# Result rows loaded inside the experts stage, and the two rows of a token added by identity products on TensorE

## The reference, cut to what matters

```python
h = h + y                                        # mixer's output
h = h + hmoe(rmsnorm(h, ln_ffn[layer]), *moe)    # experts, both layers
# hmoe: a token goes to 2 of 32 experts
#   y[token] = sum over its two experts e of
#              c[token, e] * (silu(x @ w_gate[e]) * (x @ w_up[e])) @ w_down[e]
...
return rmsnorm(h, ln_out), ...
```

## Time and profile before

| | |
|---|---|
| times of three runs | 2485.36, 2490.96 (median), 2492.52 us |
| the profiled execution's own time | 2487.45 us |
| its span, first to last instruction | 2485.8 us |
| mean granted TensorE clock | 0.915 of full |
| DMA | 409.74 MB, mean 165 GB/s |

### The profile page before, as it was taken

One profiled execution on the slowest core, in us unless ns is written; L12 is line 12 of the kernel. 1 busy time (PEld: TensorE's weight loads), 2 busy tenths in 40 slices (PEclk: granted clock), 3 DMA queues, 4 the chain that ended last, 5 costly groups with the idle time before them and its releaser, 6 DMA issues. The chain is left out here.

```text
span 2485.8 us, 44144 instructions
## 1 busy us (share of the span) xinstructions
PE 2110.0 (85%) x17339; PEld 1368.9 (55%) x17339; DVE 900.7 (36%) x1763; ACT 487.0 (20%) x1120; POOL 462.1 (19%) x548
## 2 busy tenths in 40 slices
PE   3899989998953999957987888799999975799993
PEld 2678789994752333326876555455555565233333
DVE  4655247743122111224133666434363022112123
ACT  1311112221011111101001555433343000111100
POOL 0144022220003233320002333000000001323322
PEclk7999999997865999978998999999999895899996
DMA  1498340001252999922440100555547416599952
GB/s 56 144 294 272 113 164 4 6 36 42 68 175 88 374 374 396 373 91 60 112 132 23 32 1 2 177 185 161 184 144 238 148 22 240 215 374 372 394 205 103
DMA packets 238894, 409.74 MB, mean 165 GB/s; under 512 B 56770, under 2 KB 194595, under 8 KB 212436
## 3 DMA queue, kind: packets, MB, share of 16 engines
q1 hardware_dynamic: 191140, 346.48, 38.8%
q0 software_dynamic: 40288, 56.12, 7.3%
q10 hardware_dynamic: 7264, 4.36, 0.6%
HBM read 499.03 MB, written 81.57 MB: 234 GB/s over the span
## 5 line engine op out<-in xcount | busy, mean ns | idle before, releaser
L1619 PE MATMUL banks<-slots,work 128*64 128x512 f32 x1536 | 342.6, 599 | 0.0
L2592 PE MATMUL banks<-slots 128*128 128x508 f32 x512 | 249.2, 601 | 8.7 <-ACT work L2692 7.3
L1619 PEld LDWEIGHTS banks<-slots,work 128*64 128x64 f32 x1536 | 106.2, 138 | 202.7 <-issue 201.8
L909 PE MATMUL banks<-slots 64*64 64x64 f32 x5632 | 188.9, 224 | 23.7 <-issue 7.2
L909 PEld LDWEIGHTS banks<-slots 64*64 64x64 f32 x5632 | 185.1, 140 | 25.8 <-issue 13.9
L671 PE MATMUL banks<-slots,work 128*128 128x260 f32 x768 | 175.3, 387 | 4.6 <-DMA z_state<-in_consts 4.6
L1645 PE MATMUL banks<-slots,work 128*64 128x512 f32 x768 | 175.3, 598 | 3.6 <-DVE work L1697 3.6
L2663 DVE COPY slots<-banks 64x256 f32<-64x256 f32 x256 | 109.2, 426 | 166.8 <-PE banks L2498 162.5
L1891 PE MATMUL banks<-slots,work 128*128 128x260 f32 x640 | 150.0, 397 | 18.0 <-PEq L251 16.2
L671 PEld LDWEIGHTS banks<-slots,work 128*128 128x128 f32 x768 | 145.9, 192 | 32.7 <-issue 6.2
L1331 POOL DMA_INDIRECT expert_lists<-work x20 | 19.6, 981 | 770.0 <-DVEq L251 764.5
(11 more groups left out here) (416 smaller groups left out, 3012.5 us busy)
## 6 DMA issues: line engine op xcount, KB each, us to landing
slots<-in_moe_wgate SPq DMA_DIRECT2D x64, 1024.0 KB, 9.1
slots<-in_moe_wup SPq DMA_DIRECT2D x64, 1024.0 KB, 11.6
slots<-in_moe_wdown SPq DMA_DIRECT2D x64, 1024.0 KB, 11.3
sample_cache_rows<-in_cache_kv POOLq DMA_DIRECT2D x128, 256.0 KB, 4.5
slots<-in_cache_kv SPq DMA_DIRECT2D x256, 128.0 KB, 2.2
slots<-sample_cache_rows SPq DMA_DIRECT2D x32, 512.0 KB, 6.5
slots<-sample_cache_rows SPq DMA_DIRECT2D x64, 256.0 KB, 5.0
slots<-expert_result_rows SPq DMA_DIRECT2D x8, 1024.0 KB, 9.1
```

What stands on the lines that cost most here:

```text
L909: last = nc.tensor.matmul(out[half, k, :], block_of(i, u, left)[half, k, :], moving[half, :], start=(x == 0), stop=(x == len(terms) - 1))
L1619: last = mm(c.bank[v][SEAT * j:SEAT * j + SEAT, :], xt[v][:, k, SEAT * j:SEAT * j + SEAT], weights.gate_up_of[2 * s + j][:, k], start=(k = ...
L2592: last = mm(HIDDEN[:, 0:KVH * NCMP_S], s.w1[:, u // NB, j, :], s.xt[u % 2][:, :, j % 8, first:first + NCMP_S], start=(j == 0), stop=(j == 15))
```

## The change

The loads move to the end of SP's program in `experts`, behind a wait for all scatters. POOL's own wait for the scatters and its additions go. PE multiplies both rows of a token by the identity and lets the two products accumulate in PSUM, 16 products for a tile in place of 8 transposes. DVE's additions to `h` stay as they are. The rows now lie in slots 4 to 6, and the stage `combine` is gone.

```diff
     with c.stage(f"experts{layer}") as st:
...
+        rows_loaded = [st.sem(f"rows_loaded{n}") for n in range(NTILE)]
+        summed, added = st.sem("sums_in_psum"), st.sem("sums_added")
...
         def _(sp):
...
+            sp.wait_ge(finished, PAIRS - 1)
+            for v in range(2):
+                sp.wait_ge(scattered[v], 16 * PAIRS // 2)
+            for n in range(NTILE):
+                m = P if n < TT else NB
+                two = c.expert_rows[2 * P * n:2 * P * n + 2 * m].rearrange("(p a) e -> p a e", a=2)
+                sp.dma_start(pairs[0:m, n], two).then_inc(rows_loaded[n], 16)
...
         def _(pool):
...
-            for v in range(2):
-                pool.wait_ge(scattered[v], 16 * PAIRS // 2)
...
         def _(pe):
...
+            for n in range(NTILE):
+                m = P if n < TT else NB
+                pe.wait_ge(rows_loaded[n], 16)
+                if n >= 2:
+                    pe.wait_ge(added, 2 * (n - 1))
+                for k in range(KT):
+                    for a in range(2):
+                        last = mm(c.bank[2 * (n % 2) + k // 4][:, P * (k % 4):P * (k % 4) + m],
+                                  pairs[0:m, n, a, P * k:P * k + P], c.ident[0:m, 0:m],
+                                  start=(a == 0), stop=(a == 1))
+                last.then_inc(summed, 1)
...
         def _(dve):
...
+            # the additions to h of combine, waiting for `summed`
...
-def combine(c, layer):
...
     experts(c, layer, weights)
-    combine(c, layer)
```

More of the change, by code:

```diff
@@ L1539, in experts @@
     share = c.job_lists.bitcast(F32)
+    h, NTILE = c.slot(0), TT + 1
+    pairs = c.flat(4, 3)[:, 0:NTILE * 2 * D].rearrange("p (n a e) -> p n a e", a=2, e=D)
     with c.stage(f"experts{layer}") as st:
@@ L1648, in _ @@
                 last.then_inc(finished, 1)
+            for n in range(NTILE):
[6 more added lines that the diff above has]
+                        last = mm(c.bank[2 * (n % 2) + k // 4][:, P * (k % 4):P * (k % 4) + m],
+                                  pairs[0:m, n, a, P * k:P * k + P], c.ident[0:m, 0:m], start=(a == 0), stop=(a == 1))
+                last.then_inc(summed, 1)
         @block.scalar
@@ L1707, in _ @@
                 dve.drain().then_inc(weighted, 1)
-def combine(c, layer):
[L1712 to L1721, removed]
             for n in range(NTILE):
                 m = P if n < TT else NB
[L1724 to L1751, removed]
+                dve.wait_ge(summed, n + 1)
                 for a in range(2):
```

## The result

The changed kernel takes 2482.99 us (median of 20 runs, 2476.49 to 2490.52) against 2491.95 for the kernel before (20 runs, one of them 4446.40, which doesn't move the median). The ratio is 0.9963 with a 95% interval of 0.9951 to 0.9974: 9 us faster, 6.5 to 12. I had said 21.4 us, and the time lies outside the range given. Twelve more runs gave 2488.14 against 2491.79, ratio 0.9987 (0.9972 to 1.0003), which alone would not be told from no change.

What follows compares the result with a forecast made beforehand. The stretch around combine was taken to be bound by POOL's 7.90 us drain, which nothing needs before the next stage. Load start 16.6, chain 3.8 and norm 1.0 gave 21.4 us off 2490.96: 2469 us, range 2462 to 2478.

Steps and rivals of the forecast that it cites:

- The load's start: Between experts and combine: SP's first load starts 8.3 us earlier in each layer, 16.6 us gained in all.
- rival B: At the scatters' end: the load's start doesn't move, held by what holds POOL's drain; 2486 us, chance 4%.
- The drain hidden: At the end of experts: POOL's drain runs beside the loads, over by 1099.6, some 10 us before the stage's end.
- The transfers: Loads of the rows: unchanged at 2.4 us a tile; tile 0 lands 6.1 us (layer 0) and 4.8 (layer 1) after first load.
- The clock's rise: PE's products in the sum: 4.5 us at half clock (21 products), then full clock.
- PE's work: Adding rows on PE: 16 products a tile, each costing what a transpose costs, 0.112 us at full and 0.215 at half clock.
- the chain: First load to DVE's last addition: 18.0 us for 19.96 in layer 0, 17.05 for 18.97 in layer 1; 3.8 gained.
- The norm: Norm after the additions: its products gain up to 3.3 us if the clock is still up; 1.0 us taken.
- The sum: Whole kernel: 16.6 + 3.8 + 1.0 = 21.4 us gained, giving 2469 us.
- A: Rival on PE's products: the clock stays at half and PE sets the pace; 9.1 us gained, 2482 us, chance 8%.
- C: Rival on PE's products: an f32 product costs four times a transpose; slower, 15.7 us lost a layer, 2522 us, chance 3%.

Runs made afterwards that it cites:

- the joined version with POOL's additions: Changed kernel, early loads kept, but POOL adds the two rows and PE does 8 transposes a tile, all within experts: 2487.02 us, ratio 0.9985.
- the second profile: The changed kernel run and profiled once more without an edit; its twelve runs gave 2488.14 us against 2491.79, ratio 0.9987.

## Why the prediction was wrong, step by step

*The load's start*: right. It is 8.30 us earlier in each layer, as worked out (2.16 us behind the scatter's issue in place of 10.46), and with that rival B falls. *The drain hidden*: right in the changed kernel, over 18 us ahead. What I didn't see is that this hangs on POOL having nothing left to do behind its last scatter: in the joined version with POOL's additions the drain is paid after all.

*The transfers*: right in layer 1, tile 0 at 4.75 us. In layer 0 it landed at 4.9, not at 6.1, which gave 1.2 us; why isn't shown. In the run with `combine` a stage of its own and the products alone it was 6.3 again.

*The clock's rise*: right in kind, 3.4 us of products at half clock where I took 4.5; in layer 1 of the second profile it was 6.0.

*PE's work*: this step failed. "So a product costs what a transpose costs" rested on line 1938, 64 records in 7.30 us, read as 64 products. The program has 2 x 16 products there; the row counts two instructions for each. The page of before could have told it: the transposes of line 1607 are 8 a job in the code and x384 = 48 x 8 on the page, the gate and up products of line 1619 are 16 a job and x1536, which is 48 x 16 x 2:

```profile
L1619 PE MATMUL banks<-slots,work 128*64 128x512 f32 x1536 | 342.6, 599 | 0.0
...
L1607 PE MATMUL banks<-base_constants,work 128*128 128x128 f32 x384 | 55.9, 292 | 67.5 <-DMA work<-expert_token_rows,job_lists 65.0
```

I made the same mistake with lines 360, 1346 and 1928: their 32, 16 and 64 records are 16, 8 and 32 products, and a norm has 16 products, not the 32 that I gave it ahead of the prediction.

The price of a product is 0.223 us at full and 0.427 at half clock (15 records in the window of 3.4 us, 0.213 apart). Both lie just under the upper bounds that I had from the norm's products, 0.228 and 0.455; I took the near end, 0.112 and 0.215. The mean, 19.85/80 = 0.248 us, is below the 0.27 from which I had the change come out slower, and above what the transfers hide. With it the chain is 4.9 us to the landing of tile 0, 3.4 at half clock, then 145 x 0.1117 = 16.2, and 0.5 of additions: 25.0 from the first load, as measured in layer 0. So this step brings -5.1 and -5.9 us in place of +1.9 twice. The run with half of the products confirms the rest of the sum but for the norm: 20 us gained for 21.4 said, by its profile 16.6 of the loads' start, 3.7 of the chain (3.8 said) and 0.2 of the norm (1.0 said); the run with the products alone confirms the term by itself.

The Trainium skill had it, nearly: "FP8 and Floating Point Precision", section TensorE Precision Notes, gives true FP32 four passes. I set the rule of its page "TensorE: Matmul & The Clock Gate", section Terms, aside since 0.112 stood against 0.110 per record. This trace shows a product at twice the price of a transpose, 0.223 against 0.110 us, not at 4 times.

*The norm*: wrong in sign in the first profile. The clock falls just ahead of the norm's first product and is at half until 1121.7, 6.1 us behind the norm's first product. Before, it came up within 1123 to 1126, some 3 us behind the first product at 1120.73:

```profile
1120.00:1123.00 3.00, 2.27 (x5) 1.85 (x6) 2.53 (x4) 2.94 (x5) 0.00 (x0) 0.50 0.55 155
1123.00:1126.00 3.00, 3.00 (x13) 2.49 (x12) 0.00 (x0) 0.56 (x1) 0.00 (x0) 0.85 1.13 322
```

So the norm's products take 10.32 and 10.27 in place of 8.84 and 9.03. That is 2.7 us lost where I had 1.0 gained. It differs from run to run: in the second profile it is 8.71 and 8.73, 0.4 us gained.

*The sum* with these: 16.6 - 11.0 - 2.7 = 2.9 us in the profiles of before and after, and 16.6 - 13.6 + 0.4 = 3.4 with the second profile of the changed kernel. The medians say 9.0 (6.5 to 12.2) and 3.6 (-0.7 to 7.0). Of the 6.4 us between the spans of before and after the rest lies in stretches whose code is the same. The second profile of the changed kernel, at 2484.9 us of span, doesn't have these gains, so no lasting gain elsewhere is shown. The traces bear out some 3 us as the change's own; where the rest of the 9 comes from stays open.

*The rivals*: A's time was right, 2482, by luck: the clock did rise. C's mechanism, a product dearer than a transpose, is what happened, at twice and not four times. That the change came out faster at all is due to the loads: their 16.6 us are more than the products lose.

## What to carry to other kernels

Count a row's records against the calls in the code before its mean is taken for the price of a call; here an f32 product is two records and an f32 transpose one. Before an addition moves to another engine, ask which one has time for it inside the pace that is left: PE had not, but DVE took the sums at 1.23 us a tile and the chain fell to the pace of the transfers. A drain of POOL behind many indirect DMAs is a term of its own. It comes behind POOL's last instruction of the stage, so put transfers beside it, and leave what POOL would do with their data to the next stage or to another engine.

## What the runs showed of the hardware that I had not expected

A drain of POOL takes 7.90 us at the end of the experts stage, to the nanosecond the same in both layers, though no DMA is in flight. POOL has issued 96 indirect DMAs by then, 24 gathers, 24 scatters and 48 loads of weights (the expectation above counted 80). It is paid once: with a drain of 9.0 us ahead of the last scatter, the one at the end took 0.13 us. It is paid where POOL's program ends, behind its additions too.

Where none of POOL's DMAs was in flight, the drain's time goes with the number that POOL had issued since its last drain: 0.13 us behind one, 0.96 behind 11 (the router's ten scatters and a copy), 1.61 behind 19 (plain copies, in the stage that ends at 1351.4 of the kernel before) and 7.90 behind 96, some 0.08 us for each. With DMAs in flight the drain also lasts until they land, as the drains in each job show. Why it takes 0.08 us for each isn't shown.

Adding two rows of 1024 f32 on 8 partitions took DVE 1.21 us and on 128 partitions 1.23. An f32 product of 8 moving columns costs as much as one of 128: two records of 0.112 us.
